# First block's gate projections as three split products, with h kept in two parts through the mixers

## What is computed

```python
h = rms_norm(x, norm1_g[l])
z = h @ w_in[l]
(cq, ckv, kpe, gq, gk, gv, glr, gr, su, gates) = split_in(z)
...
o_a = mla_mixer(...)      # attention, 8 heads
o_b = gla_mixer(...)      # gated linear attention
o_c = s5_mixer(...)       # a state space scan
g = jax.nn.sigmoid(gates + gate_b[l]).reshape(B, L, N_BRANCH, D)
merged = g[:, :, 0] * (o_a @ w_br_mla[l]) + g[:, :, 1] * (o_b @ w_br_gla[l]) + g[:, :, 2] * (o_c @ w_br_s5[l])
x = x + merged @ w_out[l]
```

## Time and profile before

| | |
|---|---|
| median of 3 runs | 1487.82 us (1487.55 to 1490.46) |
| the profiled execution, its own time | 1488.56 us |
| its span in the trace | 1486.8 us |
| TensorE busy | 1447.3 us, 97% |
| VectorE, ScalarE, GpSimd busy | 754.2, 697.7, 862.4 us |
| 24 gate slabs, first layer | 119.22 to 243.3 us of the span |

### The profile page before, as it was taken

One profiled execution on the slowest core, in us unless ns is written; L12 is line 12 of the kernel. 1 busy time (PEld: TensorE's weight loads), 2 busy tenths in 40 slices (PEclk: granted clock), 3 DMA queues, 4 the chain that ended last, 5 costly groups with the idle time before them and its releaser, 6 DMA issues.

```text
span 1486.8 us, 24141 instructions
## 1 busy us (share of the span) xinstructions
PE 1447.3 (97%) x9839; PEld 1293.7 (87%) x9839; DVE 754.2 (51%) x1419; ACT 697.7 (47%) x1020; POOL 862.4 (58%) x364
## 2 busy tenths in 40 slices
PE   7999999999999999999999999999999999899998
PEld 7976778989999897677898889989999988799997
DVE  4978867521112697886742221229994454321112
ACT  5644225545444564422554534455445655643444
POOL 5710000878888671000087888878885536688886
PEclk9999999999999999999999999999999999999999
DMA  6632344556666563333455667656664433466664
GB/s 194 178 103 72 98 114 128 188 172 195 187 193 189 159 177 89 85 99 100 141 191 178 194 207 241 191 156 189 194 186 127 134 108 116 140 184 187 196 185 142
DMA packets 321555, 234.48 MB, mean 158 GB/s; under 512 B 9446, under 2 KB 304901, under 8 KB 321444
## 3 DMA queue, kind: packets, MB, share of 16 engines
q1 hardware_dynamic: 321444, 232.93, 53.2%
HBM read 231.82 MB, written 1.09 MB: 157 GB/s over the span
## 4 chain that ended last, share of the span: by engine, by line
PE 83%; issue 5%; ACT 4%; POOL 3%; DVE 3%; DMA 1%; SPq 0%; DVEq 0%; POOLq 0%; ACTq 0%
PE ps L726 19%; PE ps L2049 13%; PE ps L2029 6%; PE ps L2030 6%; PE ps L2031 6%; PE ps L1112 6%; PE ps L1113 6%; PE ps L1114 6%; POOL w_lo L1340 3%; DMA raw<-in_w_in_dram 1%; PE ps L1187 1%; PE ps L2169 1%; PE ps L2183 1%; PE ps L2150 1%; PE ps L1224 1%
## 5 line engine op out<-in xcount | busy, mean ns | idle before, releaser
L1340 POOL TENSOR_TENSOR w_lo<-raw,w_hi 128x1024 fp32r<-128x1024 f32 (+1 forms) x206 | 491.4, 2402 | 478.5 <-ACT w_hi L1374 477.9
L794 POOL TENSOR_TENSOR w_lo<-raw,w_hi 128x1024 fp32r<-128x1024 f32 x154 | 370.8, 2418 | 135.5 <-ACT w_hi L816 135.1
L1374 ACT ACTIVATE w_hi<-raw 128x1024 fp32r<-128x1024 f32 (+1 forms) x206 | 217.0, 1057 | 212.2 <-PE ps L726 90.8
L1112 PE MATMUL ps<-h_hi,w_hi 128*128 128x256 f32 x864 | 243.8, 282 | 1.7 <-POOL w_lo L794 1.0
L1113 PE MATMUL ps<-h_lo,w_hi 128*128 128x256 f32 x864 | 241.4, 279 | 0.0
L1114 PE MATMUL ps<-h_hi,w_lo 128*128 128x256 f32 x864 | 241.4, 279 | 0.0
L2029 PE MATMUL ps<-h_hi,w_hi 128*128 128x256 f32 (+1 forms) x816 | 230.4, 282 | 5.4 <-DVE h_lo L1648 3.3
L2030 PE MATMUL ps<-h_lo,w_hi 128*128 128x256 f32 (+1 forms) x816 | 228.4, 280 | 0.0
L2031 PE MATMUL ps<-h_hi,w_lo 128*128 128x256 f32 (+1 forms) x816 | 228.3, 280 | 0.0
L816 ACT ACTIVATE w_hi<-raw 128x1024 fp32r<-128x1024 f32 x154 | 161.9, 1058 | 139.0 <-PE ps L1114 61.3
L2049 PE MATMUL ps<-hN,raw 128*128 128x256 f32 x768 | 174.9, 383 | 0.0
(11 more groups left out here) (340 smaller groups left out, 2442.1 us busy)
## 6 DMA issues: line engine op xcount, KB each, us to landing
raw<-in_w_in_dram SPq DMA_DIRECT2D x160, 512.0 KB, 3.8
raw<-in_w_ff_dram SPq DMA_DIRECT2D x128, 512.0 KB, 4.0
raw<-in_w_ffn_in_dram SPq DMA_DIRECT2D x44, 512.0 KB, 3.8
raw<-in_w_ffn_out_dram SPq DMA_DIRECT2D x22, 512.0 KB, 3.3
raw<-in_w_out_dram SPq DMA_DIRECT2D x16, 512.0 KB, 3.2
raw<-in_w_br_gla_dram SPq DMA_DIRECT2D x8, 512.0 KB, 3.4
raw<-in_w_br_mla_dram SPq DMA_DIRECT2D x8, 512.0 KB, 4.0
raw<-in_w_br_s_dram SPq DMA_DIRECT2D x8, 512.0 KB, 3.4
```

The lines of the kernel that those rows point to most:

```text
L794: nc.gpsimd.tensor_tensor(out=w_lo[(NS * L + i) % RING][:, 0:kt * n], in0=raw[(NS * L + i) % RING][:, 0:kt * n], in1=w_hi[(NS * L + i) % R ...
L1112: MM(out, w[0], x[0], start=first_k, stop=False, skip_group_check=skip)
L1340: nc.gpsimd.tensor_tensor(out=w_lo[(NS * l + i) % RING][:, 0:kt * n], in0=raw[(NS * l + i) % RING][:, 0:kt * n], in1=w_hi[(NS * l + i) % R ...
L1374: A_(w_hi[(NS * l + i) % RING][:, 0:kt * n], raw[(NS * l + i) % RING][:, 0:kt * n], ACT.Copy)\
```

## The change

The gate slabs become split slabs of a special kind. Their rounded part goes to four free places of `G` (`G_hi`, tiles that no gate result has yet been written to) and, for the last eight, to two buffers of `WK` (`wb_hi`); `gate_slot(k)` alternates between two places, so at most two slabs are rounded at a time. Their low part is written over `raw` itself (`raw_lo`), so the ring buffer stays taken until TensorE is done, as before. ScalarE gets 24 roundings a layer, `gate_hi(k)`, placed by hand in its list: two behind each `gate(u)` outside the attention loop, and two in each step of it. Each waits for its load and for slab k - 2 to be used. GpSimd gets 24 subtractions, TensorE `product` in the place of `product32` for these slabs. h of the first norm lives in `hg_hi` (where `hN` was) and `hg_lo` (in `WK`), which all products with it now use; `norm_h`, eight VectorE instructions, goes. `St` moves within `WK`.

```diff
@@ tiles @@
+        hg_hi = sb("hg_hi", [P, KD, T], f32r, c=norm1)
+        raw_lo = [sb(f"raw_lo{i}", [P, SLAB], f32r, c=in_place) for i in range(RING)]
+        G_hi = sb("G_hi", [P, 4, SLAB], f32r, c=gate_in)
+        hg_lo = sb("hg_lo", [P, KD, T], f32r, c=norm1)
@@ slab_parts @@
+        def gate_slot(k):
+            if k < 16:
+                return G_hi[:, (2 if k < 8 else 0) + k % 2, :]
+            return wb_hi[2 - k % 2][:, :]
@@ gpsimd @@
+                    if is_gate(i):
+                        pool.wait_ge(gh_ok.s, gh_ok(l, i - I_GATE + 1))
+                        r = (NS * l + i) % RING
+                        nc.gpsimd.tensor_tensor(out=raw_lo[r][:, :], in0=raw[r][:, :], in1=gate_slot(i - I_GATE),
+                                                op=ALU.subtract).then_inc(gl_ok.s, 1)
+                        continue
@@ scalar @@
+                def gate_hi(k):
+                    i = I_GATE + k
+                    if k == 8:
+                        act.wait_ge(qk_ok.s, qk_ok(l, 1))
+                    if k >= 2:
+                        act.wait_ge(used.s, used(l, i - 1))
+                    act.wait_ge(load_sem(l, i), load_count(l, i))
+                    A_(gate_slot(k), raw[(NS * l + i) % RING][:, :], ACT.Copy).then_inc(gh_ok.s, 1)
                     evacuate(u, I_UKV + s, [(Vt[:, :, 256 * s:256 * s + 256], pair(u % PGF), ACT.Copy, {})])
+                    gate_hi(s)
                 head_rms(0, qsq, U_QS)
                 gate(0)
+                gate_hi(2)
+                gate_hi(3)
...
                 gate(4)
+                gate_hi(10)
+                gate_hi(11)
...
                     A_(PTs[n % 2][:, 0:w], PA[3][:, 0:w], ACT.Copy).then_inc(pt_ok.s, 1)
+                    if n < 5:
+                        gate_hi(14 + 2 * n)
...
                         exps(n + 1)
+                    if n < 5:
+                        gate_hi(15 + 2 * n)
@@ vector @@
-                norm_lo(dve, stt, l, col, "norm1_g")
+                norm_lo(dve, stt, l, col, "norm1_g", hi=hg_hi, lo=hg_lo)
-                norm_h(dve, V, l, col, "norm1_g")
@@ tensor @@
+                if is_gate(i):
+                    pe.wait_ge(gl_ok.s, gl_ok(l, i - I_GATE + 1))
+                    return slab_parts(l, i)
-                        product32(l, I_GATE + i, pair(u % PGF)[:, i % 2, :], 0, P, hN).then_inc(used.s, 1)
+                        product(l, I_GATE + i, pair(u % PGF)[:, i % 2, :], 0, P, hg_hi, hg_lo).then_inc(used.s, 1)
```

More of the change, by code:

```diff
@@ L284, in build @@
         AR = sb("AR", [P, 8192], c=first)
+        sb("wk_off", [P, 40], c=first)
         split_in = ExitStack()
         wb_hi = [sb(f"wb_hi{i}", [P, SLAB], f32r, c=split_in) for i in range(3)]
-        wb_lo = [sb(f"wb_lo{i}", [P, SLAB], f32r, c=split_in) for i in range(3)]
+        wb_lo = [sb("wb_lo0", [P, SLAB], f32r, c=split_in)]
+        norm1 = ExitStack()
+        hg_lo = sb("hg_lo", [P, KD, T], f32r, c=norm1)
+        norm1.close()
+        wb_lo += [sb(f"wb_lo{i}", [P, SLAB], f32r, c=split_in) for i in (1, 2)]
         split_in.close()
@@ L506, in in_loop, with is_gate @@
             return I_LS <= i < I_LS + N_LS
+        def is_gate(i):
+            return I_GATE <= i < I_GATE + 24
+        def gate_slot(k):
+            if k < 16:
+                return G_hi[:, (2 if k < 8 else 0) + k % 2, :]
+            return wb_hi[2 - k % 2][:, :]
         def slab_parts(l, i):
+            if is_gate(i):
+                lo = raw_lo[(NS * l + i) % RING][:, :]
+                return [part.rearrange("p (k n) -> p k n", k=KD) for part in (gate_slot(i - I_GATE), lo)]
             if not in_loop(i):
@@ L652, in square_exps, with norm_lo @@
                 A_(inverse_square(b), inverse_square(b), ACT.Exp, scale=-1.0).then_inc(norm_rs.s, 1)
[L654 to L663, removed]
+        def norm_lo(dve, stt, l, gain_col, gain, at=0, hi=h_hi, lo=h_lo):
             for j in range(KD):
@@ L667, in norm_lo @@
                     dve.wait_ge(hh_ok.s, hh_ok(l, at + j // 2 + 1))
-                ins = stt(h_lo[:, j, :], ps_h(j), gain_col(gain, j), h_hi[:, j, :],
+                ins = stt(lo[:, j, :], ps_h(j), gain_col(gain, j), hi[:, j, :],
                           ALU.mult, ALU.subtract)
@@ L1391, in h_rounded @@
                             act.wait_ge(ht_ps.s, ht_ps(l, NP * k + j // 2 + 1))
[L1392 removed]
+                        ins = A_(hi[:, j, :], ps_h(j), ACT.Copy, scale=col(gain, j))
                         if j % 2:
@@ L1407, in _ @@
                 act.wait_ge(cols_ok.s, cols_ok(l, 1))
-                h_rounded(0, "norm1_g", 2)
+                h_rounded(0, "norm1_g", 2, hg_hi)
                 for u in range(10):
@@ L2046, in product32 @@
                 for k in range(kt):
-                    if fresh is not None and k % 2 == 0:
-                        pe.wait_ge(hf_ok.s, hf_ok(l, NP * fresh + k // 2 + 1))
                     last = MM(out, w[:, k, c0:c0 + n], x[:, x0 + k, :], start=k == 0, stop=k == kt - 1)
@@ L2074, in token_major @@
                         x, first_k = 4 * half + k, half == 0 and k == 0 and b == 0
-                        MM(out[:, b, :], h_hi[:, x, tb], w[0][:, k, :], start=first_k, stop=False, skip_group_check=True)
-                        MM(out[:, b, :], h_hi[:, x, tb], w[1][:, k, :], start=False, stop=False, skip_group_check=True)
-                        last = MM(out[:, b, :], h_lo[:, x, tb], w[0][:, k, :], start=False,
+                        MM(out[:, b, :], hg_hi[:, x, tb], w[0][:, k, :], start=first_k, stop=False, skip_group_check=True)
+                        MM(out[:, b, :], hg_hi[:, x, tb], w[1][:, k, :], start=False, stop=False, skip_group_check=True)
+                        last = MM(out[:, b, :], hg_lo[:, x, tb], w[0][:, k, :], start=False,
                                   stop=half == 1 and k == 3, skip_group_check=True)
@@ L2114, in _ @@
                     out = pair((U_Z + t // 2) % PGF)[0:n, t % 2, :]
-                    product(l, i, out, 0, n, h_hi, h_lo, fresh=None if t else 0).then_inc(used.s, 1)
+                    product(l, i, out, 0, n, hg_hi, hg_lo, fresh=None if t else 0).then_inc(used.s, 1)
                     if t == 11:
-                        pe.wait_ge(hf_ok.s, hf_ok(l, NP))
                         pe.wait_ge(lat_sq.s, lat_sq(l, 1))
```

29 lines of the change are left out of this document (23 added, 6 removed).

## The result

The changed kernel takes 1547.43 us (median; 1545.89 to 1550.03) against 1488.88 us before (1487.55 to 1490.46): 1.0395 times as long, with a 95% interval from 1.0374 to 1.0415. The direction was forecast, the size was not: +58.5 us instead of +14. The profiled execution took 1550.03 us, its span is 1548.2.

The account below looks back on a forecast made before the run. The gates were taken to run at TensorE's pace; per layer 19.7 us lost less 17.4 saved gave +2.3, so 2 x 2.3 + 10.0 for the clock = 14.6, forecasting 1502 us, range 1490 to 1510.

Parts of the forecast that it names:

- TensorE's saving: Gate slabs on TensorE: a split slab takes 2.83 us, 0.72 less than an unsplit one, 17.4 us a layer.
- The chain behind an eviction: Between gate pairs: eviction, rounding, then subtraction take 4.47 us; TensorE loses what other work does not cover.
- the head sums: Ahead of two sets of head sums: roundings delay logarithms that free TensorE's banks, costing 0.67 and 0.89 us.
- The failed step: Throughout the layer's gate stretch: VectorE's instructions keep the lengths of the earlier profile's rows; no loss counted for this.
- the walk: Place-by-place sum of TensorE's losses through a layer: 19.7 us lost against 17.4 saved, +2.3 us a layer.
- nothing ahead of slab 6: At slab 6: the linear attention's outputs cover the wait for the low part, so TensorE loses 0.
- 5.93 for the loop: Attention loop: odd slabs' roundings stand behind exponentials; waits at slabs 15, 19, 21, 23 and two transposes, 5.93 us.
- The sum: Whole kernel: 2 x 2.3 us of net waits plus 10.0 for the clock, 14.6 us slower.
- The clock: Two 4.47 us waits in each layer lower TensorE's clock: four falls at 2.5 us, 10.0 us, all on the path.
- The rival of more harm: GpSimd's subtraction grows to 2.94 us, waits grow 5.4 in all, two more clock falls cost 5.0: 1513 us; chance 0.09.
- the rule that the prediction cited: Trainium skill on TensorE's clock: a kernel waiting between short bursts is throttled at each wait and pays for warm-up.
- norm_h: Removing its 3.21 us of VectorE work brings nothing, as its successor's chain waits 6.70 us for ScalarE later.

Follow-up runs that it names:

- experiment 3: Changed kernel with GpSimd subtracting only 128 of a gate slab's 1024 columns, the third product's other seven eighths reading the high part: 1476.63 us, 0.9917.
- experiment 1: Kernel before plus 24 unrelated full-length GpSimd subtractions a layer, of the halves of hN, nothing else of the change: 1550.98 us, 1.0424.
- experiment 4: Changed kernel with the third product reading the high part, so GpSimd subtracts in full but no gate slab waits for its low part: 1525.34 us, 1.0246.
- experiment 7: Changed kernel with 30 overwritten TensorE products put into the waits ahead of slabs 10 and 12 of each layer: 1544.60 us, 1.0364.
- experiment 8: Kernel before plus 24 unrelated GpSimd copies of 1024 columns a layer, one operand read, in place of subtractions: 1490.29 us, 1.0009.
- experiment 9: Kernel before plus 24 unrelated GpSimd subtractions a layer, the first 14 cut to 128 columns, full length only in the attention loop: 1521.95 us, 1.0225.

## Why the prediction was wrong

- **TensorE's saving** was sized too high. From one start to the next, the 24 gate slabs of the first layer take 85.7 us in the kernel before and 72.1 in that of experiment 3, where the clock hardly falls: 3.00 us a slab, 2.91 in a pair and 2.93 to 3.14 alone, where I had 2.83 for all. A lone split slab costs what the branch slab of the earlier trace rows showed, and taking 0.11 off it was wrong. That is 13.6 instead of 17.4 us a layer, 7.6 us of the miss in two layers.
- **The chain behind an eviction** was right, and is the part to copy. Forecast 2.45, 4.47 and 4.47 us ahead of slabs 8, 10 and 12, measured 2.38, 4.57 and 4.30; slab 4 0.65 for 0.80, the head sums 0.41 and 0.50 for 0.67 and 0.89. The links of the 4.57, in the changed kernel's timeline, answer:

```profile
185.82 0.84 ACT L1407 ACTIVATE G<-ps,cols 128x256 f32<-128x256 f32 x2 [2.23 <-PE ps L2082]
...
186.55 2.00 ACT L1497 ACTIVATE G_hi<-raw 128x1024 fp32r<-128x1024 f32 x2
...
187.68 5.40 POOL L1357 TENSOR_TENSOR raw_lo<-raw,G_hi 128x1024 fp32r<-128x1024 f32 x2 [7.64 <-ACT G_hi L1497]
...
190.35 0.58 PE L2080 MATMUL ps<-hg_hi,G_hi 128*128 128x256 f32 x1 [4.57 <-POOL raw_lo L1357]
```

- **The failed step** is one that the prediction made without a word: in its walk VectorE's instructions kept their lengths from the rows, although GpSimd, at 0.00 in the earlier trace rows, was to work beside them for 58 us a layer. From it came nothing ahead of slab 6 (5.24 measured), nothing at slab 5 (1.28) and at the linear attention's outputs (0.90), and 5.93 for the loop (8.9, of which 7.5 are VectorE's). Idle time in the walk: 29.1 us a layer instead of 19.7. Experiments 1, 3 and 4 show the cause: with the subtractions cut short the same kernel takes 1476.6 us, and unrelated ones alone bring the kernel before to 1551.0.
- **The sum** of the first layer then comes out: 29.1 idle (forecast 19.7) plus 13.5 for the lower clock (forecast 5.0) less 13.6 saved (forecast 17.4) is 29.0 us, where the stretch grew by 29.1 and the forecast had 7.3.
- **The clock.** Forecast four falls in all for 10.0 us. The sizes were right for two of them a layer: slabs 10 and 12 took 5.4 and 5.3 us, 2.4 and 2.3 over a slab at full clock. But the waits for VectorE (5.24, and in the loop 1.35 and 2.12, 1.87 and 2.12, each two close together) bring three more, and TensorE lost some 13.5 us a layer: its busy time in the stretch stayed (148.94 and 148.82) although the slabs need 13.6 less. As time it is worth less than that: experiment 7 took two falls a layer away and got back 3 of 9.6 us. "All of it is on the path since TensorE is last there" was wrong as soon as VectorE was last.
- **The rival of more harm** had the right pair of engines and the wrong one of them as the victim. It let GpSimd's subtraction go to its longest, 2.94, for 5.4 us in all. The mean did rise, to 2.57, but the longest reached 4.43, for GpSimd is held as well. So it came to slab 5's 1.28 us (timeline of the changed kernel):

```profile
140.86 6.73 POOL L1357 TENSOR_TENSOR raw_lo<-raw,G_hi 128x1024 fp32r<-128x1024 f32 x2 [7.68 <-ACT G_hi L1497]
...
141.34 4.02 DVE L1700 SCALAR_TENSOR_TENSOR MD<-MD,cols,G 64x2048 f32<-64x2048 f32 x1
145.38 4.36 DVE L1697 TENSOR_TENSOR MD<-fr,G 32x2048 f32<-32x2048 f32 x1
```

The two engines take turns here. VectorE's first step waits for the first subtraction, the second subtraction for that step, VectorE's second step for the second subtraction. The 2.94 in the earlier trace rows is the sign that I misread. It is this one, in the kernel before, with the VectorE instructions ahead of it:

```profile
259.05 2.35 DVE L1645 TENSOR_TENSOR wb_lo<-raw,wb_hi 128x1024 fp32r<-128x1024 f32 x2
260.73 2.94 POOL L1340 TENSOR_TENSOR w_lo<-raw,w_hi 128x1024 fp32r<-128x1024 f32 x1 [178.83 <-ACT w_hi L1374]
```

The subtraction began 0.67 us before VectorE was done with two SBUF operands, and lasted 0.54 us too long: the hold in the other direction. And early in the same trace the victim is VectorE:

```profile
21.89 2.39 POOL L1340 TENSOR_TENSOR w_lo<-raw,w_hi 128x1024 fp32r<-128x1024 f32 x1 [0.79 <-ACT w_hi L1374]
...
22.49 0.17 DVE L1687 CAST smi<-ps 128x16 int32<-128x16 f32 x1
22.70 1.62 DVE L1688 CAST sms<-smi 128x16 f32<-128x16 int32 x1
24.35 0.61 DVE L1648 SCALAR_TENSOR_TENSOR ps<-sms,ps 128x16 f32<-128x16 f32 x3
```

A cast of 16 columns from SBUF takes 1.62 us and ends with the subtraction, while the cast from PSUM just ahead takes 0.17. A cleaner pair is the scalar step of line 1683, also 16 columns from SBUF: 0.17 us at 21.65, with no subtraction beside it, and 1.63 in the second layer at 503.09, up to the end of the subtraction there. Most of what VectorE does beside GpSimd in the kernel before has an operand in PSUM, but not all. This group of the second block, with both operands in SBUF, has a mean of 1.37 us:

```profile
L977 DVE SCALAR_TENSOR_TENSOR Up<-fr 128x256 f32<-128x256 f32 x8 | 10.9, 1365 | 18.3 <-ACT fr L822 18.1
```

Without a subtraction beside it, one of them takes 0.42 us. So the hold, and its size, stood in the trace of before. The Trainium skill ("SBUF — State Buffer", "Who interferes with whom") states the rule: VectorE and GpSimd share one pair of SBUF ports, an instruction of VectorE with two SBUF inputs contends with a GpSimd instruction that reads SBUF, and the loser blocks for the whole of the other. It also names copies, casts and scalar steps of VectorE, in modes that take both ports; whether the steps above ran in one, no trace shows. It speaks against this change more than the rule that the prediction cited, and no run here speaks against it.
- **norm_h** brought nothing, as said: the changed kernel reaches the stretch at 93.66, the other at 93.15.

Left open: why 21 us of held VectorE cost nothing in experiment 8 and 33 us cost 33 in experiment 9. Shorter holds (1.4 against 2.5 us) that VectorE's slack between two steps absorbs would explain it; no run separates length from place.

## What to carry to other kernels

Work on GpSimd is not free because GpSimd is idle. List what VectorE does at that time, and count each instruction with two operands in SBUF, and each scalar step, cast or copy from SBUF to SBUF, as held for the rest of GpSimd's; 24 subtractions of 2.4 us cost VectorE 32 us a layer here. Look in the trace for one form of VectorE instruction with two lengths, the longer beside GpSimd: it shows the hold before the change is made. And a price for a lower TensorE clock belongs into a sum only while TensorE is the last engine there.

## What the runs showed of the hardware

- GpSimd's subtraction holds VectorE's instructions with two SBUF operands (0.69 to 2.8 us), its scans, and even a scalar step on 128x2 elements from SBUF to SBUF (0.17 to 2.25 us). Those with an operand in PSUM (0.68 us) aren't touched, nor are a reciprocal of 128x2 from SBUF (0.17 us, in the changed kernel at 204.35) and ScalarE's evictions (0.47 us in both kernels).
- The hold goes both ways: a subtraction of 1024 columns, 2.36 us alone, took up to 4.43 beside VectorE, one of 128 columns up to 2.14.
- A GpSimd copy of 1024 columns, one operand read, takes 1.04 us alone and holds VectorE too.
- A GpSimd subtraction of 128 columns takes 0.46 us, of 256 at best some 0.7 and on average 0.97, of 1024 2.36: small pieces are dear.
- The granted clock was 0.50 after a wait of 4.57 us and still 1.00 after one of 2.38; the wait filled up to 0.95 us kept 1.00. It was also 0.50 from 241 to 247 us, around waits of 1.35 and 2.12 us with 1.1 us of products between them.
